# Two more load buffers for the expert weights of a fused two-block layer, and two expert loads issued earlier

## The reference: what is computed

```python
x = first_block(...)    # SSD + latent attention, cross attention, experts, final norm
return second_block(x, ...)

# first_block, in its order
u = rms_norm(h, norm_mix)
merged = sigmoid(gate_ssd) * y_ssd + sigmoid(gate_mla) * y_mla
h = h + merged @ w_o
h = h + memory_cross_attention(rms_norm(h, norm_xattn), rms_norm(mem, norm_mem), w_xq, w_xkv, w_xo)
h = h + hierarchical_moe(rms_norm(h, norm_moe), ...)   # 32 experts, 2 for each token
return rms_norm(h, norm_final)

# hierarchical_moe
hg = einsum('td,edf->tef', t, w_gate)      # w_gate, w_up: 32 x 1024 x 256
hu = einsum('td,edf->tef', t, w_up)
act = silu(hg) * hu * combine[:, :, None]
y = einsum('tef,efd->td', act, w_down)     # w_down: 32 x 256 x 1024
```

## Time and profile before

| | |
|---|---|
| median of three runs | 1107.22 us (1103.17 to 1111.86) |
| profiled execution, span from first to last instruction | 1106.8 us (no time beside the span is given for it) |
| TensorE busy | 1021.5 us, 92% |
| VectorE, ScalarE busy | 622.6 us (56%), 516.9 us (47%) |
| mean granted TensorE clock | 0.974 of full speed |
| DMA over the span | 240.96 MB, 218 GB/s |
| DMA from about 480 to 720 us | 99 to 102% busy in nearly all windows of 10 us, some 420 GB/s |

### The profile page before, as it was taken

One profiled execution on the slowest core, in us unless ns is written; L12 is line 12 of the kernel. 1 busy time (PEld: TensorE's weight loads), 2 busy tenths in 40 slices (PEclk: granted clock), 3 DMA queues, 4 the chain that ended last, 5 costly groups with the idle time before them and its releaser, 6 DMA issues.

```text
span 1106.8 us, 19429 instructions
## 1 busy us (share of the span) xinstructions
PE 1021.5 (92%) x8574; PEld 941.1 (85%) x8574; DVE 622.6 (56%) x828; ACT 516.9 (47%) x701; POOL 19.4 (2%) x24
## 2 busy tenths in 40 slices
PE   7999989899999899999997676788999999999998
PEld 6999978899889899899665443478999999999998
DVE  6887677765565784544111101068994665545566
ACT  5576576745555554442211110158566564443443
POOL 0000020001000000000000000000000000000000
PEclk9999999999999899998998888899999999999999
DMA  7665343446223555299999999964430355555441
GB/s 279 231 242 191 137 155 115 150 150 238 80 77 115 193 188 191 99 365 406 384 420 421 420 420 421 420 267 157 162 114 11 153 213 206 190 191 190 163 143 39
DMA packets 34871, 240.96 MB, mean 218 GB/s; under 512 B 4064, under 2 KB 4448, under 8 KB 6368
## 3 DMA queue, kind: packets, MB, share of 16 engines
q1 hardware_dynamic: 33264, 232.54, 55.1%
q0 software_dynamic: 1232, 6.99, 1.8%
q10 hardware_dynamic: 288, 0.15, 0.1%
HBM read 238.58 MB, written 1.08 MB: 217 GB/s over the span
## 4 chain that ended last, share of the span: by engine, by line
PE 68%; DVE 12%; DMA 9%; ACT 7%; issue 3%; SPq 2%; DVEq 0%; ACTq 0%
PE ps L457 15%; PE ps L459 15%; PE ps L458 15%; DVE wlo L1976 4%; PE ps L530 4%; PE ps L1226 4%; DMA xlo<-in_c_weights 3%; ACT whi L1325 3%; DMA xhi<-in_c_weights 3%; DMA wr<-in_c_weights 2%; PE ps L1192 2%; SPq L2933 2%; PE ps L1253 1%; PE ps L1266 1%; PE ps L929 1%
## 5 line engine op out<-in xcount | busy, mean ns | idle before, releaser
L1976 DVE TENSOR_TENSOR wlo<-raw,whi 128x2048 fp32r<-128x2048 f32 (+1 forms) x119 | 269.5, 2266 | 141.1 <-ACT whi L1325 141.1
L457 PE MATMUL ps<-XUh,whi 128*128 128x256 f32 x992 | 282.3, 285 | 9.2 <-DVE wlo L1976 8.4
L459 PE MATMUL ps<-XUh,wlo 128*128 128x256 f32 x992 | 278.3, 281 | 0.0
L458 PE MATMUL ps<-XUl,whi 128*128 128x256 f32 x992 | 278.2, 280 | 0.0
L1325 ACT ACTIVATE whi<-raw 128x2048 fp32r<-128x2048 f32 (+1 forms) x119 | 223.5, 1880 | 61.9 <-PE ps L459 61.9
L457 PEld LDWEIGHTS ps<-XUh,whi 128*128 128x128 f32 x992 | 187.3, 189 | 11.3 <-issue 7.7
L459 PEld LDWEIGHTS ps<-XUh,wlo 128*128 128x128 f32 x992 | 189.4, 191 | 0.0
L458 PEld LDWEIGHTS ps<-XUl,whi 128*128 128x128 f32 x992 | 187.5, 189 | 0.3
L1226 PE MATMUL ps<-wr,Xg 128*32 128x256 f32 x464 | 57.6, 433 | 6.2 <-DMA wr<-in_c_weights 4.6
L2855 DVE SCALAR_TENSOR_TENSOR sphs<-sphs,wsl,ps 128x256 f32<-128x256 f32 x8 | 3.8, 480 | 99.0 <-ACT sphs L1941 99.0
L1941 ACT ACTIVATE sphs<-ps 128x256 f32<-128x256 f32 x8 | 3.1, 383 | 102.1 <-PE ps L1226 102.1
(11 more groups left out here) (619 smaller groups left out, 2377.4 us busy)
## 6 DMA issues: line engine op xcount, KB each, us to landing
raw<-in_c_weights SPq DMA_DIRECT2D x141, 1024.0 KB, 4.9
wr<-in_c_weights SPq DMA_DIRECT2D x42, 1024.0 KB, 26.4
xhi<-in_c_weights SPq DMA_DIRECT2D x13, 1024.0 KB, 26.1
xlo<-in_c_weights SPq DMA_DIRECT2D x13, 1024.0 KB, 26.3
acb<-sums POOLq DMA_DIRECT2D x4, 1024.0 KB, 5.1
T<-in_c_weights SPq DMA_DIRECT2D x4, 1024.0 KB, 26.8
T8b<-in_c_weights SPq DMA_DIRECT2D x4, 1024.0 KB, 26.4
raw<-in_c_weights SPq DMA_DIRECT2D x4, 576.0 KB, 3.7
```

Source lines behind the costliest of these rows:

```text
L457: pe.matmul(ps, h(k), xh(k), start=start and k == 0, stop=False, skip_group_check=loose)
L458: pe.matmul(ps, h(k), xl(k), start=False, stop=False, skip_group_check=loose)
L459: t = pe.matmul(ps, l(k), xh(k), start=False, stop=stop and k == kt - 1, skip_group_check=loose)
L1976: dve.tensor_tensor(l[:, 0:n], r, h[:, 0:n].bitcast(F32), ALU.subtract).then_inc(*did("w_lo", "split", i))
```

## The change

- `extra0` and `extra1`, two buffers of 8 KB in each partition, are added, at the head of `stock`: 23 buffers in place of 21. e0 and e1 go into them and wait for nothing; every later expert piece is two places on in the list.
- SP issues e0 and e1 between the second and the third piece of xo, the last projection of the cross attention.
- The memory comes from the descriptor scratch (1 KB in place of 16 KB in each partition), from `masks`, which moves into the shared region and is loaded behind the experts, just ahead of `reset`, and from `sm`, of which the two halves now lie closer together.
- Because 96 pieces fill 21 and 23 places differently, other places hold the last pieces.

```diff
+    extra = [sb(f"extra{i}", [128, PIECE], F32) for i in range(2)]
     raw = [sb(f"raw{i}", [128, PIECE], F32) for i in range(NRAW)]
...
-    masks, vec = sb("masks", [128, 896], U8), sb("vec", [128, 256], F32)
+    vec = sb("vec", [128, 256], F32)
...
-    sm = sb("sm", [128, 128], F32)
+    sm = sb("sm", [128, 64], F32)
...
-    stock = [("raw", (moe0 + j) % NRAW) for j in range(2)] + [("wr", j) for j in (3, 4, 0, 1, 2, 5)]
+    stock = [("extra", 0), ("extra", 1)]
+    stock += [("raw", (moe0 + j) % NRAW) for j in range(2)] + [("wr", j) for j in (3, 4, 0, 1, 2, 5)]
...
-    reset = R("reset", [128, 1024], F32, 70 * KB)
+    reset, masks = R("reset", [128, 1024], F32, 70 * KB), sb("masks", [128, 896], U8, rbase + 75 * KB)
...
-        pool.dma_start(posi[:, :], I["positions"].broadcast_to([128, 256])).then_inc(*did("tables", by=16))
-        pool.dma_start(masks[:, :], I["c_masks"]).then_inc(*did("tables", "dma", "tables", by=16))
+        pool.dma_start(posi[:, :], I["positions"].broadcast_to([128, 256])).then_inc(*did("tables", "dma", "tables", by=16))
...
         w.wait_ge(*at_("moe", "added", 3))
+        pool.dma_start(masks[:, :], I["c_masks"]).then_inc(*did("reset", by=16))
         pool.dma_start(reset[:, :], I["c_reset"]).then_inc(*did("reset", "dma", "reset", by=16))
...
-        for i in range(4, len(pieces)):
+        late = first["xo"] + 2
+        for i in itertools.chain(range(4, late), (moe0, moe0 + 1), range(late, moe0), range(moe0 + 2, len(pieces))):
             load(i)
...
-    nc = bacc.Bacc("TRN2", target_bir_lowering=False, num_devices=1)
+    nc = bacc.Bacc("TRN2", target_bir_lowering=False, num_devices=1, dynamic_dma_scratch_size=1024)
```

More of the change, by code:

```diff
@@ L1 @@
+import itertools
 import numpy as np
@@ L301, in build @@
     spare = {("raw", j): raw[j] for j in range(NRAW)}
+    spare.update({("extra", j): extra[j] for j in range(2)})
     spare.update({("wr", j): R(f"wr{j}", [128, PIECE], F32, (24 + 8 * j) * KB) for j in range(6)})
@@ L1651, in act_program @@
             for hd in range(4):
-                t = act.activation(Px[j][:, hd, :], Px[j][:, hd, :], ACT.Exp, bias=sm[:, 64 * j + 8 + hd:64 * j + 9 + hd],
-                                   accum_out=sm[:, 64 * j + 16 + hd:64 * j + 17 + hd])
+                t = act.activation(Px[j][:, hd, :], Px[j][:, hd, :], ACT.Exp, bias=sm[:, 32 * j + 8 + hd:32 * j + 9 + hd],
+                                   accum_out=sm[:, 32 * j + 16 + hd:32 * j + 17 + hd])
             t.then_inc(*did("xa_act", "xa", "exp", j))
@@ L2396, in dve_program @@
         for j in range(2):
-            sj = sm[:, 64 * j:64 * j + 64]
+            sj = sm[:, 32 * j:32 * j + 32]
             w.wait_ge(*at_("xa_sc", j))
```

## The result

| kernel | median of its runs | lowest to highest | profiled span |
|---|---|---|---|
| before | 1105.32 us (20 runs) | 1101.73 to 1111.86 | 1106.8 us |
| changed | 1099.42 us (20 runs) | 1088.86 to 1104.96 | 1097.6 us |

The ratio is 0.993, with a 95% interval of 0.9913 to 0.9948: 5.9 us by medians (7.1 by means), where 2.8 was forecast. The sign and the class (within 1%) came as forecast, and 1099.42 lies at the lower edge of the range, but the gain is twice the sum's.

A forecast was written before the change was run, and what follows sets the result against it. It took the expert stretch to be bound by load bytes once the pipe is full. Terms -5.0 us (two pieces fewer) and +2.2 us (late hz loads) gave -2.8 us: median 1107.2 to 1104.4 us, range 1099 to 1110 us.

The forecast's parts named there:

- Bounded by bytes in the expert stretch; two pieces fewer are 5.0 us: Expert loads: 69 pieces instead of 71 land after the first refill, so the stretch ends 5.0 us sooner.
- Two early loads cost nothing: Between xo's second and third pieces: both loads fit in the 20.8 us gap, delaying nothing; cost nothing.
- hz's loads wait for L1301: Second block's start: hz's first two loads wait for the last downs; TensorE 1.2 us late, ScalarE 2.2 us late.
- The last ups, the scatter and the last downs follow e91 at their old distance: End of the expert stretch: everything after the last up load moves with it, so the last downs end 5.0 us earlier.
- The term +2.2: Second block's start: ScalarE's late split of hz's second piece gives back 2.2 us of the gain, through VectorE.
- All 5.0 us stay: Rival at the second block's start: hz's loads land in time or VectorE's order has room; 1102.2 us, chance 0.15.
- Nothing comes of it: Rival: pipe runs dry before 560 us, saving no bytes; 1107.2 us, or 1109.4; chance 0.17 (nothing or a little worse).
- TensorE's clock: Rival: TensorE's new pause before L530 brings half clock, costing about 1.8 us; 1106.2 us, chance 0.08.
- Slower, by the small scratch: Rival: GpSimd's 1 MB loads go in eight parts with 1 KB scratch, 11.4 us late; 1115.8 us, chance 0.08.

The follow-up runs named there:

- e1: Not a run: the second of the 96 expert pieces, which the changed kernel loads into an added buffer between xo's second and third piece.
- no_early: The changed kernel with its 23 buffers, but the first two expert pieces issued behind xo's: 1099.99 us, ratio 0.9934 to the kernel before.
- layout21: The changed kernel's memory layout (1 KB scratch, masks late, smaller sm) with 21 buffers and the old load order: 1107.58 us, ratio 1.0003 to the kernel before.
- before_again: The kernel before, run once more unchanged in the second session: 1105.53 us, ratio 0.9988.
- after_again: The changed kernel, run once more as it is in the first session: 1099.73 us, ratio 0.9932 to the kernel before.

## Why the prediction was wrong

- **Bounded by bytes in the expert stretch; two pieces fewer are 5.0 us**: right. 4.9 us between kernels of the same layout, and the cut and added pieces show the mechanism by itself. (The Trainium skill, "DMA: Bandwidth & Descriptors", the section on the anatomy of one DMA, gives 4.8 by the slope of a fit that it made on loads issued by GpSimd, where these are SyncE's; measured 4.9, between 4.8 and 5.0.)
- **Two early loads cost nothing**: right, xo's third piece went at 464.22. But they aren't needed: no_early is as fast. What I called fetching in the empty time also happens after xo's loads.
- **hz's loads wait for L1301**: right, down to the rows: issued at 721.22 (722.9 forecast, and 1.2 us of the difference lie ahead of the first up), ScalarE late by 2.4 us and TensorE by 1.6 (2.2 and 1.2 forecast).
- **The step that failed: "The last ups, the scatter and the last downs follow e91 at their old distance".** They don't. From the start of the last 64 ups to the end of the last downs it was 16.0 us before (711.91 to 727.91) and 14.8 in the changed kernel (706.39 to 721.22). The same delay that makes hz late lets the load queue run dry at the turn, and the branch there no longer waits as long for its packet: 5.07 us for 5.99, and 1.6 us less in the means of nine profiles each. The term +2.2 is right as a wait and wrong as a sum: net it is +0.7 us, or -0.2 if the half clock of three profiles before the change counts as spared, which is not shown. The second `wlo` was forecast 2.8 us earlier; the profile has it at 737.23, which is 4.3 us earlier, of which 1.2 came ahead of the first up.
- With that the sum is -4.2 to -5.1 us, just short of the interval of the first comparison, whose near end, 0.9948, is 5.7 us. The rest, from 0.8 us by its medians to 3.8 by the means of all sessions, is the open part above; no term of the prediction stood for it, and no run shows its cause.
- **The rivals.** "All 5.0 us stay" was the nearest, though not for its reason: the loads are late. "Nothing comes of it" fell with the column. "TensorE's clock" fell: behind the new pause ahead of L535 (1.2 to 1.6 us) the windows stay at a granted clock of 1.00 in all nine profiles that have it, and the half clock at this place came in three profiles with the old pause of 2.4 to 2.7 us. (The Trainium skill, "TensorE: Matmul & The Clock Gate", the part on the HAM clock gate, has idleness lead to half clock; these three profiles agree, the other six with that pause did not show it.) "Slower, by the small scratch" fell: layout21 1.0003, and a 1 MB load of GpSimd still lands after 4.8 us, beside 5.1 in the earlier trace rows:

```profile
acb<-sums POOLq DMA_DIRECT2D x4, 1024.0 KB, 4.8
```

## What to carry to other kernels

Where a stretch is bound by loads, count bytes behind the moment at which the pipe fills: every buffer of 1 MB was worth 2.4 to 2.5 us, from 17 to 23, and every piece cut short 2.0 us. When a transfer is delayed, do not only ask who waits for it; ask who runs faster while it is not there: here a branch, of which the wait is seen only in the sequencer's own row. And cut several profiles of each kernel at the same marks before a few microseconds are put down to a stage: two executions of one kernel differed here by 7 us ahead of the first mark (before, before_again), and by 4.5 behind the last (changed, after_again).

## What the hardware did that I had not expected

- A branch on TensorE that skips code took 5.9 to 6.2 us under a full load queue (nine profiles) and 4.0 to 5.1 us with the queue running dry (nine). In all 18 it ended 2.5 us after the start of a 16 KB packet of the instruction queue.
- Two matmul paces at the same granted clock of 1.00: 1021 and 1061 matmuls in 120 us. Which stretch gets which changes from one execution of a kernel to the next: between 60 and 70 us eleven profiles have 90 or 91 matmuls in 10 us and seven have 87 or 88; before is slow there and before_again fast, and both are slow from 930 us on.
- A descriptor scratch of 1 KB served 1 MB loads of GpSimd without a measurable cost.
